# Pairs of heads in the forgetting attention, one output bank and a new order of rounds in the recurrent stage

## The reference, cut to what matters

```python
log_f = jax.nn.log_sigmoid(f + b_forget)
cum = jnp.cumsum(log_f, axis=1).transpose(0, 2, 1)
s = einsum('bhqd,bhkd->bhqk', qb, kh) + cb[..., :, None] - cum[:, :, None, :]
a = softmax(where(causal_mask(start, T), s, NEG_INF)); o = einsum('bhqk,bhkd->bhqd', a, vh)
```

```python
decay = jnp.exp(-jnp.exp(w_log))      # = exp(-exp(-0.5) * sigmoid(w0 + tanh(xw) @ w2))
k = k * (1.0 + (a - 1.0) * k_a)
Sa = einsum('bhij,bhj->bhi', S, a_t)
S = S * w_t[:, :, None, :] + Sa[..., None] * b_t[:, :, None, :] + v_t[..., None] * k_t[:, :, None, :]
y = einsum('bhij,bhj->bhi', S, r_t)
```

## Time and profile before

| | before |
|---|---|
| median of 3 runs | 3559.74 us (3558.8 to 3567.33) |
| profiled execution | 3568.84 us |
| its span, first to last instruction | 3567.0 us |
| mean granted TensorE clock | 0.950 |
| PE busy | 3258.5 us (91%) |
| weight loads busy | 2591.9 us (73%) |
| DVE busy | 2027.3 us (57%) |
| ACT busy | 1301.2 us (36%) |
| POOL busy | 373.1 us (10%) |

### The profile page before, as it was taken

One profiled execution on the slowest core, in us unless ns is written; L12 is line 12 of the kernel. 1 busy time (PEld: TensorE's weight loads), 2 busy tenths in 40 slices (PEclk: granted clock), 3 DMA queues, 4 the chain that ended last, 5 costly groups with the idle time before them and its releaser, 6 DMA issues.

```text
span 3567.0 us, 51794 instructions
## 1 busy us (share of the span) xinstructions
PE 3258.5 (91%) x21458; PEld 2591.9 (73%) x21458; DVE 2027.3 (57%) x3572; ACT 1301.2 (36%) x2140; POOL 373.1 (10%) x332
## 2 busy tenths in 40 slices
PE   6898899999898999998988988879999889989998
PEld 4677778887685678886766766567777777768886
DVE  5445457663432467654556347588778763554444
ACT  3234242222323342223343135365555433333221
POOL 0001100000000000000000000065455420000000
PEclk9898899999998999999999889999999999999999
DMA  3220034432231134432311120211111103232231
GB/s 129 62 71 1 13 107 139 143 128 92 71 95 36 36 118 137 142 122 78 107 48 54 49 90 18 71 51 46 40 43 39 47 6 106 83 106 95 95 100 66
DMA packets 298344, 274.78 MB, mean 77 GB/s; under 512 B 10368, under 2 KB 289024, under 8 KB 297344
## 3 DMA queue, kind: packets, MB, share of 16 engines
q1 hardware_dynamic: 293856, 256.07, 22.3%
q10 hardware_dynamic: 4256, 15.40, 1.2%
HBM read 265.16 MB, written 6.29 MB: 76 GB/s over the span
## 4 chain that ended last, share of the span: by engine, by line
PE 80%; DVE 10%; ACT 5%; issue 3%; POOL 1%; DMA 1%; DVEq 0%; ACTq 0%; SPq 0%; POOLq 0%
PE ps L95 78%; DVE f L107 3%; DVE f L101 2%; DVE r L101 2%; PE ps L98 1%; ACT f L88 1%; ACT f L92 1%; ACT r L92 1%; DVE f L104 1%; ACT f L89 1%; DVE f L113 1%; POOL f L101 1%; ACT L88 1%; DVE f L110 1%; DVE r L107 0%
## 5 line engine op out<-in xcount | busy, mean ns | idle before, releaser
L95 PE MATMUL ps<-r,r 128*128 128x512 f32 x10368 | 2455.5, 397 | 114.2 <-DVE r L101 78.7
L95 PEld LDWEIGHTS ps<-r,r 128*128 128x128 f32 x10368 | 1942.9, 192 | 569.3 <-issue 141.5
L95 PE MATMUL ps<-f,f 64*64 64x64 f32 (+10 forms) x10170 | 757.0, 265 | 166.8 <-ACT f L92 49.4
L101 DVE TENSOR_TENSOR r<-f,r 128x1024 fp32r<-128x1024 f32 (+2 forms) x621 | 655.8, 1063 | 422.7 <-ACT r L92 412.1
L95 PEld LDWEIGHTS ps<-f,f 64*64 64x64 f32 (+3 forms) x10170 | 574.4, 155 | 338.1 <-issue 164.8
L92 ACT ACTIVATE r<-f 128x1024 fp32r<-128x1024 f32 (+2 forms) x548 | 506.8, 937 | 754.6 <-PE ps L95 637.6
L107 DVE SCALAR_TENSOR_TENSOR f<-f,f,f 128x128 f32<-128x128 f32 (+3 forms) x630 | 374.6, 600 | 26.4 <-ACT f L88 7.3
L101 POOL TENSOR_TENSOR f<-f,f 128x512 f32<-128x512 f32 (+2 forms) x272 | 326.7, 1214 | 498.5 <-ACT f L88 229.9
L101 DVE TENSOR_TENSOR f<-ps,f 128x512 f32<-128x512 f32 (+5 forms) x331 | 178.5, 551 | 337.1 <-PE ps L95 327.6
L92 ACT ACTIVATE f<-ps 128x256 f32<-128x256 f32 (+4 forms) x417 | 181.0, 449 | 518.1 <-PE ps L95 369.5
L88 ACT ACTIVATE f<-ps 128x512 f32<-128x512 f32 (+4 forms) x214 | 117.7, 556 | 590.5 <-PE ps L95 590.2
(11 more groups left out here) (34 smaller groups left out, 722.5 us busy)
## 6 DMA issues: line engine op xcount, KB each, us to landing
f<-in_w_mlp_up SPq DMA_DIRECT2D x32, 1024.0 KB, 6.0
f<-in_w_mlp_down SPq DMA_DIRECT2D x32, 1024.0 KB, 6.3
f<-in_w_ff SPq DMA_DIRECT2D x32, 1024.0 KB, 5.2
f<-in_w_in SPq DMA_DIRECT2D x26, 1024.0 KB, 4.9
f<-in_w_ada SPq DMA_DIRECT2D x48, 512.0 KB, 3.9
f<-in_w_in SPq DMA_DIRECT2D x40, 512.0 KB, 3.5
f<-in_w_in_even SPq DMA_DIRECT2D x12, 1024.0 KB, 5.1
f<-in_w_in_odd SPq DMA_DIRECT2D x12, 1024.0 KB, 5.2
```

Source lines behind the costliest of these rows:

```text
L95: return self.e.matmul(out, l, r, start=first, stop=last)
L101: return self.e.tensor_tensor(out, a, b, op)
```

## The change

In the forgetting attention the units run in pairs: heads 2a and 2a+1, for each block of queries. In every second round PE first makes the two bias matmuls, one on partitions 0 to 39 and one on 64 to 103, and then the two products of q and k; each pair adds up in its own bank. `lf`, `L`, `Rb` and `one40` have a second copy of their rows from partition 64 on for this, and the row tiles of both heads are made together. Two output banks are held at a time.

In the recurrent stage:
- The r, k and v halves run in rounds 4 to 7, 10 and 11 (`PROJ`).
- DVE's 12 taps run in the rounds of `ROUND_OF`, by the method `taps`: none in 2, 7 and 8, and two in 0, 3 and 11.
- The i-products and ta-products of a chunk go into one bank. PE waits for its own matmuls between them, ACT copies the sum to `yn`, and DVE has no `out` step.
- The scaling by -exp(-0.5) moves into the scales of ACT's exponentials. `KK` is made on ACT, as are the copies of AV and U0.
- B and KK lie beside each other (`BK`), and so do lw and L (`lwL`); one DVE product of 512 columns stands for two of 256 in pD and in pE. lw and L swap places as the scaled keys and removal vectors.

```diff
@@ -2083,7 +2083,7 @@
         self.o = K.h
         self.X = Split(K, lambda j: K.hh_r[:, j, :], lambda j: K.h_r[:, j, :])
         self.out = OutProj(K, "odd.out", K.A["w_out_odd"][0], self.X, x_done)
-        self.units = [(h, qt) for h in range(8) for qt in range(4)]
+        self.units = [(2 * a + b, qt) for a in range(4) for qt in range(4) for b in range(2)]
...
         for u, p in waves(32, 6):
             h, qt = self.units[u]
             km, qs = (qt + 1) * 128, slice(qt * 128, qt * 128 + 128)
             if p == 0:
-                pe.wait_ge("fox_row", h + 1)
-                b = self.bank["s", u] = K.ps.take(pe, ("fox_max", u + 1))
-                pe.mm(K.ps.t[b][:, 0:km], self.q[:, h, qs], self.k[:, h, 0:km], True, False)
-                K.mm_done(pe.mm(K.ps.t[b][:, 0:km], self.L[0:40, qs], self.rh[h % 2][0:40, 0:km], False, True), ("fox.s", u))
+                if h % 2:
+                    continue
+                pe.wait_ge("fox_row", h + 2)
+                for w in range(2):
+                    r = slice(64 * w, 64 * w + 40)
+                    b = self.bank["s", u + w] = K.ps.take(pe, ("fox_max", u + w + 1))
+                    pe.mm(K.ps.t[b][:, 0:km], self.L[r, qs], self.rh[w][r, 0:km], True, False)
+                for w in range(2):
+                    b = self.bank["s", u + w]
+                    K.mm_done(pe.mm(K.ps.t[b][:, 0:km], self.q[:, h + w, qs], self.k[:, h + w, 0:km], False, True), ("fox.s", u + w))
             elif p == 3:
                 pe.wait_ge("fox_n", u + 1)
                 b = self.bank["t", u] = K.ps.take(pe, ("fox_pt", u + 1))
...
         dve.settle()
         dve.wait_ge("fox_zero", 1)
         s3 = blocks(self.sp_, 4)
-        for o in (0, 32):
+        for o in (0, 32, 64, 96):
...
         p = K.ps.t[self.bank["cum"]]
-        dve.cp(self.L[32:40, :], p[32:40, :]).then_inc(S("fox_cum"), 1)
-        dve.cp(self.Rb[0:8, :], p[0:8, :]).then_inc(S("fox_cum"), 1)
+        for o in (0, 64):
+            dve.cp(self.L[o + 32:o + 40, :], p[o + 32:o + 40, :]).then_inc(S("fox_cum"), 1)
+            dve.cp(self.Rb[o:o + 8, :], p[o:o + 8, :]).then_inc(S("fox_cum"), 1)
         dve.fence()
         mask, one = K.c("mask"), K.c("one40")
         for u, p in turns(32, (0, 1, 2, 5)):
...
-            if p == 0 and qt == 0:
-                if h >= 2:
-                    dve.wait_ge("mm", K.done["fox.s", 4 * (h - 2) + 3])
-                dve.ts(self.rh[h % 2][0:40, :], self.Rb[0:40, :], one[0:40, h:h + 1], None, MUL, None).then_inc(S("fox_row"), 1)
+            if p == 0 and qt == 0 and h % 2 == 0:
+                for w in range(2):
+                    r = slice(64 * w, 64 * w + 40)
+                    if h:
+                        dve.wait_ge("mm", K.done["fox.s", u - 2 + w])
+                    dve.ts(self.rh[w][r, :], self.Rb[r, :], one[r, h + w:h + w + 1], None, MUL, None).then_inc(S("fox_row"), 1)
...
+    ROUND_OF = (5, 6, 9, 10, 11, 11, 0, 0, 1, 3, 3, 4)
...
+
+    def taps(self, r):
+
+        n, k = r // 12, r % 12
+        m = n + 1 if k >= 5 else n
+        for t in range(self.TAPS):
+            if self.ROUND_OF[t] == k and 0 <= m < 8:
+                yield m, "tap", t
...
-        self.early = [[al(2, H2)] + [al(H2) for _ in range(5)] for _ in range(4)]
+        self.early, self.pairs = [], []
+        for _ in range(4):
+            AR, BK, lwL, E = al(2, H2), al(2, H2), al(2, H2), al(H2)
+            self.early.append([AR, BK[:, 0, :], BK[:, 1, :], lwL[:, 0, :], lwL[:, 1, :], E])
+            self.pairs.append((BK, lwL))
...
-    DVE = ("c", "out", "xy", "tm", "fin", "tap", "ct", "p", "g", "i0", "cf", "proj")
+    PROJ = (4, 5, 6, 7, 10, 11)
+    DVE = ("c", "xy", "tm", "fin", "turn", "ct", "p", "g", "i0", "cf", "proj")
...
-                if k in ("cf", "cf1", "tap"):
+                if k == "turn":
+                    for m, what, q in self.cf.taps(r):
+                        yield m, m, 0, "cf" + what, q
+                elif k in ("cf", "cf1", "tap"):
...
-                    if r < 84 and 4 <= r % 12 < 10 and (not split or r % 2 == (k == "proj1")):
+                    if r < 84 and r % 12 in self.PROJ and (not split or r % 2 == (k == "proj1")):
                         n = r // 12 + 1
-                        yield 2 * n, n, 0, "proj", r % 12 - 4
+                        yield 2 * n, n, 0, "proj", self.PROJ.index(r % 12)
...
-                for j, srcs in enumerate(((AR[:, 0, :], L), (lw, v))):
+                for j, srcs in enumerate(((AR[:, 0, :], lw), (L, v))):
...
-                    self.bank["i", u] = K.ps.hold(pe, ("rw_yi", u + 1))
-                    self.bank["ta", u] = K.ps.hold(pe, ("rw_out", u + 1))
-                bi = P[self.bank["i", u]]
+                    self.bank["o", u] = K.ps.hold(pe, ("rw_out", u + 1))
+                else:
+                    pe.wait_ge("mm", K.done["rw.ta", u, l - 1])
+                o = P[self.bank["o", u]]
...
                 for m in range(2):
                     h = half_of(m)
-                    t = pe.mm(bi[h, cs], S2[h, :], AR[h, 1, cs], True, True)
-                if l == 3:
-                    K.mm_done(t, ("rw.i", u))
+                    t = pe.mm(o[h, cs], S2[h, :], AR[h, 1, cs], True, False)
+                K.mm_done(t, ("rw.i", u, l))
             elif p == "ct":
-                w, pb, cs, ba = l // 2, half_of(l % 2), col(l), P[self.bank["ta", u]]
+                w, pb, cs, o = l // 2, half_of(l % 2), col(l), P[self.bank["o", u]]
...
                 K.mm_done(t, ("rw.st", u, l))
+                pe.wait_ge("mm", K.done["rw.i", u, l])
                 for m in range(2):
                     h = half_of(m)
-                    pe.mm(ba[h, cs], tm[pb, 3, w, h], M[pb, 2 * m + w, 1, 1, :], True, False)
-                    t = pe.mm(ba[h, cs], Yb[pb, col(2 * m + w)], M[pb, 2 * m + w, 0, 1, :], False, True)
-                if l == 3:
-                    K.mm_done(t, ("rw.ta", u))
+                    pe.mm(o[h, cs], tm[pb, 3, w, h], M[pb, 2 * m + w, 1, 1, :], False, False)
+                    t = pe.mm(o[h, cs], Yb[pb, col(2 * m + w)], M[pb, 2 * m + w, 0, 1, :], False, True)
+                K.mm_done(t, ("rw.ta", u, l))
             elif p == "out":
-                K.ps.leave(self.bank["i", u])
-                K.ps.leave(self.bank["ta", u])
+                K.ps.leave(self.bank["o", u])
...
+                act.wait_ge("rw_a", u + 1)
+                act.f(KK, B, ACT.Identity, scale=col("k_a"), bias=self.omk[:, n:n + 1]).then_inc(S("rw_kk"), 1)
             elif p == "pB":
                 act.wait_ge("mm", K.done["rw.n", u])
                 act.f(self.rs[u % 2], P[self.bank["n", u]][:, 0:4], ACT.Sqrt).then_inc(S("rw_root"), 1)
                 act.wait_ge("rw_L", u + 1)
-                act.f(E, L, ACT.Exp).then_inc(S("rw_E"), 1)
+                act.f(E, L, ACT.Exp, scale=-self.E05).then_inc(S("rw_E"), 1)
             elif p == "pC":
                 act.wait_ge("rw_l2", u + 1)
-                act.f(lw, lw, ACT.Exp).then_inc(S("rw_l3"), 1)
+                act.f(lw, lw, ACT.Exp, scale=-self.E05).then_inc(S("rw_l3"), 1)
                 act.wait_ge("rw_E", u + 1)
-                act.f(L, L, ACT.Exp, scale=-1.0).then_inc(S("rw_l4"), 1)
+                act.f(L, L, ACT.Exp, scale=self.E05).then_inc(S("rw_l4"), 1)
...
+                if l == 1:
+                    act.wait_ge(self.nth("x", u), 5 * (u // 2) + 1)
+                    act.cp(AV, P[self.bank["tr", u]][:, H2:512]).then_inc(S("rw_av"), 1)
...
+                act.wait_ge("mm", K.done["rw.u0", u])
+                act.cp(A1, P[self.bank["u0", u]][:, 0:H2]).then_inc(S("rw_u0"), 1)
             elif p == "out":
-                act.wait_ge("mm", K.done["rw.i", u])
+                act.wait_ge("mm", K.done["rw.ta", u, 3])
...
-                act.cp(self.yn[:, hs], P[self.bank["i", u]][:, 0:H2]).then_inc(S("rw_yi"), 1)
+                act.cp(self.yn[:, hs], P[self.bank["o", u]][:, 0:H2]).then_inc(S("rw_out"), 1)
...
-                dve.own(dve.ts(lw, lw, -self.E05, None, MUL, None))
-                dve.wait_ge("rw_a", u + 1)
-                dve.own(dve.ts(KK, B, col("k_a"), self.omk[:, n:n + 1], MUL, ADD))
-                dve.settle()
                 dve.e.tensor_tensor_scan(L, K.c("reset")[:, 0:H2], lw, 0.0, MUL, ADD).then_inc(S("rw_L"), 1)
+                dve.wait_ge("rw_kk", u + 1)
                 dve.own(dve.tt(KK, KK, k, MUL))
...
-                dve.own(dve.tt(KK, KK, L, MUL))
                 dve.wait_ge("rw_k", u + 1)
                 dve.wait_ge("mm", K.done["rw.ns", u])
                 dve.tt(AR[:, 0, :], AR[:, 0, :], P[self.bank["ns", u]][:, 0:H2], MUL).then_inc(S("rw_kn"), 1)
                 dve.wait_ge("rw_kn", u + 1)
                 dve.own(dve.tt(B, B, AR[:, 0, :], MUL))
                 dve.settle()
-                dve.own(dve.tt(B, B, L, MUL))
+                dve.own(dve.tt(BK, BK, L.unsqueeze(1).broadcast_to((128, 2, H2)), MUL))
```

(16 more changed lines are left out.)

31 lines of the change are left out of this document (17 added, 14 removed).

## The result

The changed kernel takes 3541.73 us in the median of five runs (3529.22 to 3544.5), the kernel before 3563.13 in five beside it (3558.8 to 3577.89): a ratio of 0.992, 95% interval 0.9896 to 0.9946 (the quotient of the two medians is 0.994). So it is faster, by 21 us between the medians, where 42 were forecast. The time lies 24 us above the forecast of 3518: outside its own range of 3502 to 3533, inside the wide range of 3488 to 3548, and inside the 3534 to 3547 of rival (b). The profiled execution took 3544.47 us, its span 3542.7, its mean clock 0.951.

A forecast was written before the change was run, and what follows sets the result against it. PE bounds the kernel, waiting for late DVE in the recurrent stage. Holes 29, lead-in 2, tail 4 and attention 7 sum to 42 us off the median 3559.74: 3518, own range 3502 to 3533, wide range 3488 to 3548.

The forecast's parts named there:

- rival (b): Recurrent stage: PE's wait only moves to rounds 8 and 9, the clock falls as before; 3534 to 3547; chance 0.20.
- The bound and the hole: Recurrent stage, a period: 68.7 us of full-speed PE work, 6.0 waits, 2.4 slow clock; hole in rounds 10 and 11.
- DVE sheds 7.4 a period: Recurrent stage: scalings, copies, output addition and merged products take 3.7 us a block off DVE, 7.4 of 60 a period.
- 0.8 put back: Rounds 7 to 9: half of the scalings' 1.60 us may be POOL's and pass to the next DVE op.
- The walk: Waits from round 7 to tm: 2.2 + 0.8 + 1.2 = 4.2 us a period for 6.0, a gain of 1.8.
- The clock holds: Recurrent stage: waits cut in two, each well short of 4.0 us, keep the clock up, another 2.4 a period.
- (a): Recurrent stage: the hole closes entirely, 8.4 us in each of 7; 3488; chance 0.14.
- The lead-in: Recurrent stage, rounds -12 to -1: DVE's, with one tap less and two halves moved; 2 us gained.
- The tail: End of the recurrent stage, 93 us: DVE sheds about 9, is late in less than half; 4 us gained.
- The one bank and the waits for PE's own products: Recurrent stage, output bank: PE's waits for its own earlier matmuls cost nothing, at most 1.2 us a period.
- The attention: Forgetting attention: paired bias matmuls save 11.8, copy waits cost 4.6, slow start +1.9, setup 2.4: 7 us, bounds -7, +14.
- The slow first stretch: Forgetting attention, first 1.3 heads at half clock: the saving doubles there, 1.9 us more.

The follow-up runs named there:

- run 4: Changed kernel with POOL's additions of the convolution's products cut to 8 of 512 columns, output incomplete: 3486.36 us, ratio 0.9768.
- run 6: Changed kernel with POOL's products and additions moved out of rounds 6 to 8, all still computed: 3528.81 us, ratio 0.9875.
- run 10: Changed kernel with POOL's work moved out of rounds 6 to 8 and the forgetting attention's output product one round later: 3507.03 us, ratio 0.9818.
- run 2: Changed kernel with the projection halves back in rounds 4 to 9: 3547.34 us, ratio 0.995.
- run 3: Changed kernel with DVE's taps back in the old order, one a round: 3549.26 us, ratio 0.9935.
- run 8: Changed kernel with the bias matmuls of both heads on partitions 0 to 39: 3540.28 us in one run.

## Why the prediction was right in sign and half in size

**The bound and the hole: right.** PE's 68.7 us of full-speed work a period are close to what run 4 shows when nothing holds it (67.7, in a period of 68.0), and the waits in rounds 10 and 11 are gone.

**DVE sheds 7.4 a period: short.** DVE near 53 was said; it is 55.2 to 56.9, so 5 went. Of the means by form, the scan rose from 1096 ns to 1485 and the shifts and taps from 932 to 956: (8 x 0.389 + 60 x 0.024) / 4 = 1.1 us a period handed back, for 0.8 put back in the walk. The difference of lw and L gives back another 0.7 (943 ns for the 581 of its form before). The products of 512 columns have a mean of 0.69 us where the sum took 0.73; the 1.3 that the prediction says it takes is in no term of that sum.

**The walk: its main step failed, and the sum came near by luck.** 4.2 us of waits were forecast and 3.45 measured. But PE gets going behind its second wait 14.53 to 14.56 us after the start of the half of round 7 in all four periods, whatever its clock: DVE sets that time. In the first period, at full clock, PE waited 2.27 and 2.57 us for it, 4.84 in all, where the walk had 2.2 + 0.8; in the second and third the slow clock stretched the work between the waits from 2.85 us to 4.95 and left 0.22 of the second. The wait of 1.2 before tm isn't there. The term that failed is the 0.8 put back for POOL: DVE took 11.2 us (2580.40 to 2591.58) for what the walk put at 8.1, so 3.1 came back, 2.5 of it in the scan, the two products and the shift. The main wait also stands in round 8 at the third chunk, not in round 9 alone: I walked from 2595.77 as one stretch and held PE only to its end, while `sa` of each chunk is a deadline of its own.

**The clock holds: this step failed.** The forecast took all of 2.4 us a period for it. PE's work exceeds 68.7 us by 0.9, 3.5, 3.7 and 1.0 us in the four periods, 2.3 in the mean. About half of that is hidden, as it falls between the two waits. Behind the second wait the rest of the period takes 60.05, 60.33, 60.47 and 58.67 us; against the last, the slow clock costs 1.4, 1.7 and 1.8, which is 1.2 in the mean of the four. So of the 1.5 us by which the mean period of 74.4 misses the forecast 72.9, the clock is 1.2; the waits at full clock are 0.8 longer than said (5.0, those of the first period, for 4.2), and PE's work at full speed is some 0.5 shorter, an estimate from the last period (68.2). Over the seven groups 16.1 us were gained for 29. What held the step in its place was the argument that waits well short of 4.0 leave the clock alone; a single wait of 2.27 us was followed by 9.38 us of work at 0.52. In run 6, with waits of at most 0.8, the grant is 1.00 throughout. Why the clock fell behind the first wait in three periods and only behind the second in the other was not found.

**The rivals.** Rival (b) is the nearest, in time and in mechanism: the waits moved to rounds 8 and 9, 4.84 us at full clock for 5.64 before, and the clock falls as before. It had a chance of 0.20, the forecast with its own range 0.56. Its price was not what happened, 0 to 13 us for the groups where 16.1 were gained, and 13 for the rest where 8.2 were. Runs 6 and 10 (71.4 a period) stand between the forecast's 72.9 and (a)'s 68.6.

**The lead-in: this step failed too.** 2 us were to be gained and 2.3 were lost: PE's waits in it are 15.39 us for 14.53, and its work takes 57.54 us for 56.07, at a clock of 0.88 for 0.93. PE waits 7.21 us once, where it had waits of 1.60 and 4.71 before (timeline of the changed kernel):

```profile
2314.16 21.25 POOL L101 TENSOR_TENSOR f<-f,f 128x512 f32<-128x512 f32 x13 [50.41 <-ACT f L88]
...
2325.64 0.72 ACT L88 ACTIVATE f<-f,f 128x512 f32<-128x512 f32 x1 [0.68 <-POOL f L101]
2327.04 0.72 ACT L88 ACTIVATE f<-f,f 128x512 f32<-128x512 f32 x1 [0.68 <-POOL f L101]
2327.67 1.04 ACT L92 ACTIVATE r<-f 128x1024 fp32r<-128x1024 f32 x1
...
2328.74 2.16 DVE L101 TENSOR_TENSOR r<-f,r 128x1024 fp32r<-128x1024 f32 x1 [5.68 <-ACT r L92]
...
2331.05 5.46 PE L95 MATMUL ps<-r,r 128*128 128x512 f32 x12 [7.21 <-DVE r L101]
```

Read upwards: PE waits for the low part of a weight piece, DVE for its high part, and ACT rounds that piece only at 2327.67, since its products ahead in the queue wait for POOL to free their two buffers. The lead-in is less DVE's than POOL's: with the small additions it takes 60.95 us. I had costed an edit of the halves' order by taps alone, and not what their rounding stands behind on ACT. The order explains only part of the loss: with the old halves (run 2) the lead-in takes 71.99.

**The tail:** 2.6 for 4. In the stretch as cut DVE is busy 4.0 us less (35.89 to 31.87); 9 had been put for a longer one.

**The one bank and the waits for PE's own products: nothing, as said.** In the middle 280 us of the stage the list of PE's waits has none for itself in the changed kernel, 0.5 us in run 6, and 1.0 in 250 us of run 3.

**The attention: right, for partly wrong reasons.** The steady part was 9.9 us a head and is 9.0, as forecast: 7.3 us over the eight heads for 11.8 - 4.6 = 7.2. The waits are 0.37, 0.58, 0.58 and 0.69 us a pair of heads, 2.22 for 2.4. Running together is worth 2.13 for 2.94. Most of the gap is filled by something the forecast did not have: the old order's work is 19.81 us less 1.26 of waits = 18.55, against run 8's 20.12 - 2.22 = 17.90. That may be the grouping of the products by kind; no run has it alone. Ahead of the loop -2.3 for -2.4 (first matmul of the loop at 1118.04, then at 1120.38). The slow first stretch made the difference of 3 us: it was to save 1.9 and saved 5.1. Before, it was 24.95 us of work at 0.60; after, in windows:

```profile
1120.38:1136.00 15.62, 14.78 (x48) 8.02 (x49) 5.47 (x25) 6.02 (x18) 0.00 (x0) 0.67 0.00 1
```

That is 0.40 x 24.95 = 10.0 us lost to the clock, and now 0.33 x 14.78 = 4.9. Why the grant rose sooner was not tested.

**Behind the stage** 2.1 us were lost at a clock that fell at the end of the stage and was low for 17 us instead of 10, the last 5 of them behind it; run 6 has 614.89 there. No work of the change lies in it.

**The account:** 12.9 (the seven groups) + 4.3 (lead-in) + 1.4 (tail) + 2.1 (behind) - 3.0 (attention) = 17.7 us of the 42 not seen, leaving 24.3 in the profiled execution, by which its span fell.

## What to carry to other kernels

When VectorE (DVE) is lightened beside a busy GpSimd (POOL), price the next operations of its queue by a run in which the other is silent, and look first where the other works: here moving POOL's additions gave 11.7 us of the stage, where rewriting DVE's operations and the order had given 16.3. Walk a late engine deadline by deadline, each operation that PE waits for, not from one end of a stretch to the other. An operation taken out ahead of others moves them in time: look at what the other engine does where they land. And cost the slow clock behind a wait, but only the part that no second wait for the same late engine hides: waits of 0.8 us cost none here, those of 2.3 and 2.6 us cost 1.2 us a period.
